# The last tile of a gate projection issued among the first score groups of a stick-breaking attention

## What is computed

```python
def _sb_layer(x, k, v, norm_g, w_in, w_out):
    q, g = split(_rms(x, norm_g) @ w_in)        # two halves of 1024 columns
    o = _stick_breaking(q, k, v)                # 16 heads of 64
    return x + (o * silu(g)) @ w_out

# stick-breaking, per block of 128 query rows, mask: kpos < qpos
z = q @ k.T * scale
log_beta, log_1mb = log_sigmoid(z), where(mask, log_sigmoid(-z), 0)
suffix = reversed_cumsum(log_1mb) - log_1mb
a = where(mask, exp(log_beta + suffix), 0)
o = a @ v
```

## Time and profile before

| | |
|---|---|
| median of 3 runs | 2435.43 us (2435.22 to 2443.52) |
| the profiled execution | 2447.21 us; span 2445.4 us, mean granted TensorE clock 0.99 |
| PE busy | 2346.2 us (96%) |
| DVE busy | 1492.6 us (61%) |
| ACT busy | 994.6 us (41%) |
| POOL busy | 209.0 us (9%) |
| DMA | 116.02 MB, mean 47 GB/s |

### The profile page before, as it was taken

How to read it: one execution, slowest core, us unless ns; L and a number is a source line. 1 busy time by engine, 2 the same in 40 slices (tenths; PEclk the granted TensorE clock), 3 DMA queues, 4 the chain that set the end, 5 groups by cost and what they waited for, 6 DMA issues and landing times.

```text
span 2445.4 us, 30312 instructions
## 1 busy us (share of the span) xinstructions
PE 2346.2 (96%) x12882; PEld 1255.3 (51%) x12882; DVE 1492.6 (61%) x1880; ACT 994.6 (41%) x1498; POOL 209.0 (9%) x258
## 2 busy tenths in 40 slices
PE   7999989999999999999999977899999999989999
PEld 5445444444444444444544455654444446777764
DVE  6898855644644455587732388865534405988951
ACT  5245344221212122433332578842323215878841
POOL 0001030000000000533301101022000000000000
PEclk9999999999999999999999999999999999999999
DMA  4010000201110101003111000021131200010021
GB/s 183 35 70 35 1 35 35 103 35 69 41 63 35 69 35 69 32 6 138 35 69 35 34 2 1 1 104 35 69 138 35 70 1 1 1 36 1 1 87 52
DMA packets 50343, 116.02 MB, mean 47 GB/s; under 512 B 2402, under 2 KB 7835, under 8 KB 49824
## 3 DMA queue, kind: packets, MB, share of 16 engines
q1 hardware_dynamic: 48472, 105.40, 12.1%
q10 hardware_dynamic: 1736, 8.68, 0.9%
HBM read 101.49 MB, written 12.58 MB: 47 GB/s over the span
## 4 chain that ended last, share of the span: by engine, by line
PE 79%; DVE 12%; ACT 7%; issue 1%; DMA 1%; POOL 0%; SPq 0%; DVEq 0%; ACTq 0%
PE PS L72 76%; PE PS L75 4%; ACT RG L81 3%; DVE RG L107 2%; DVE R L93 2%; DVE mx L110 2%; DVE R L101 2%; ACT OV L84 2%; DVE RG L101 1%; DVE RG L93 1%; DMA RG<-in_a_w_in 1%; ACT R L81 1%; DVE scl L110 1%; DVE oss L110 1%; ACT mx L81 0%
## 5 line engine op out<-in xcount | busy, mean ns | idle before, releaser
L72 PE MATMUL PS<-R,RG 128*128 128x512 f16 (+1 forms) x5472 | 1164.7, 374 | 7.5 <-DVE R L93 3.4
L72 PEld LDWEIGHTS PS<-R,RG 128*128 128x128 f16 (+1 forms) x5472 | 542.6, 103 | 625.3 <-issue 10.2
L72 PE MATMUL PS<-RG,R 128*128 128x512 f16 x2880 | 632.6, 380 | 3.6 <-DVE R L101 3.1
L72 PEld LDWEIGHTS PS<-RG,R 128*128 128x128 f16 x2880 | 281.9, 98 | 335.4 <-issue 5.2
L81 ACT ACTIVATE R<-PS,scl 128x512 f32<-128x512 f32 (+1 forms) x192 | 126.7, 686 | 700.4 <-PE PS L72 630.9
L101 DVE SCALAR_TENSOR_TENSOR R<-PS,scl,R 128x512 f32<-128x512 f32 (+1 forms) x208 | 148.6, 745 | 147.2 <-PE PS L72 122.6
L107 DVE TENSOR_TENSOR_SCAN RG<-RG 128x127 f32<-128x127 f32 (+7 forms) x128 | 168.4, 1342 | 92.1 <-ACT RG L81 91.9
L101 DVE SCALAR_TENSOR_TENSOR RG<-RG,scl 128x4096 f16<-128x4096 f32 (+2 forms) x52 | 190.6, 3664 | 54.4 <-ACT RG L81 54.4
L72 PE MATMUL PS<-R,OV 128*128 128x64 f32 (+2 forms) x1456 | 198.8, 279 | 7.2 <-DVE R L93 4.8
L81 ACT ACTIVATE RG<-RG,scl 128x4096 f16<-128x4096 f32 (+2 forms) x52 | 158.6, 3050 | 89.1 <-DVE scl L113 89.1
L110 DVE TENSOR_REDUCE scl<-RG 128x1 f32<-128x4096 f32 (+2 forms) x39 | 155.0, 3975 | 64.4 <-DMA RG<-in_a_w_in 25.3
(11 more groups left out here) (128 smaller groups left out, 1554.4 us busy)
## 6 DMA issues: line engine op xcount, KB each, us to landing
RG<-in_w_ff SPq DMA_DIRECT2D x16, 2048.0 KB, 8.2
RG<-in_a_w_in SPq DMA_DIRECT2D x8, 2048.0 KB, 8.6
xspill<-R ACTq DMA_DIRECT2D x2, 4096.0 KB, 15.6
RG<-in_w_kv SPq DMA_DIRECT2D x4, 2048.0 KB, 8.0
RG<-in_b_w_in SPq DMA_DIRECT2D x4, 2048.0 KB, 8.0
RG<-in_w_in SPq DMA_DIRECT2D x3, 2048.0 KB, 7.9
R<-in_x SPq DMA_DIRECT2D x8, 512.0 KB, 8.0
RG<-in_w_out SPq DMA_DIRECT2D x2, 2048.0 KB, 7.8
```

The costliest lines, as they stand in the source:

```text
L72: return self.engine.matmul(*a, **k) if self.engine else Nothing()
```

## The change

The seven first gate tiles stay where they are; the seventh is pinned to banks 6 and 7. The eighth tile's halves are issued in banks 6 and 7 behind the scores of groups 1 and 2, so that the order on PE is scores 0, scores 1, `("g2", 7, 0)`, scores 2, `("g2", 7, 1)`, scores 3, and then transposes of group 0. As the weights of tile 38 are still read while groups 0 and 1 are at work, their 1 - beta goes to `EB[2]` and `EB[3]` (`kept(u)`), and ACT waits for joins 0 and 1 before it writes the beta of groups 2 and 3 there.

On ACT the eighth tile's two Silu stand behind the beta of group 2, the first copy, `turned(0, 0)`, right behind them, then 1 - beta of group 3, copy (0, 1), beta of group 3, copies (1, 0), (1, 1) and (2, 0). On DVE the gating of group 0 stands behind the join of group 3 rather than ahead of its scans. The loops are the same from group 4 on.

```diff
-            for t in range(NT):
+            for t in range(NT - 1):
                 for c in range(2):
-                    product_n(38 + c, t, ("g2", t, c))
+                    product_n(38 + c, t, ("g2", t, c), bank=6 + c if t == NT - 2 else None)
...
             scores([0])
-            for u in range(N + 2):
-                if u + 1 < N:
+            scores([1])
+            product_n(38, NT - 1, ("g2", NT - 1, 0), bank=6)
+            scores([2])
+            product_n(39, NT - 1, ("g2", NT - 1, 1), bank=7)
+            for u in range(1, N + 2):
+                if u == 1:
+                    scores([3])
+                elif 2 < u < N - 1:
                     if sb_groups[u + 1][0] < 4:
                         scores([u + 1])
                     elif u % 2:
```

```diff
+        def kept(u):
+            return EB[2 + u] if u < 2 else EC[u % 3]
...
+            for u in range(N + 3):
+                if u != 3:
+                    gated(u - 3)
...
-                        back = EC[u % 3][:, w * x + 1:w * x + w][:, ::-1]
+                        back = kept(u)[:, w * x + 1:w * x + w][:, ::-1]
...
                     e.tensor_tensor(eb, eb, ec, ALU.mult).then_inc(*sig("joined_b").up(u))
+                if u == 3:
+                    gated(0)
```

```diff
-                turned(u - 2, 1)
+                if u == 3:
+                    turned(0, 1)
+                if u > 3:
+                    turned(u - 2, 1)
                 if u < N:
+                    if u in (2, 3):
+                        e.wait_ge(*sig("joined_b").at(u - 2))
...
-                turned(u - 1, 0)
+                if u == 2:
+                    gate_silu(NT - 1)
+                    turned(0, 0)
+                if u == 3:
+                    turned(1, 0)
+                    turned(1, 1)
+                if u > 2:
+                    turned(u - 1, 0)
```

More of the change, by code:

```diff
@@ L1822, in vector, with gated @@
             N = len(sb_groups)
-            for u in range(N + 3):
-                if u >= 3:
-                    i, hs = sb_groups[u - 3]
+            def gated(u):
+                if u >= 0:
+                    i, hs = sb_groups[u]
                     if hs[-1] % 8 == 7:
@@ L1843, in vector @@
                     w = width(i)
-                    eb, ec = by_head(EB[u % 4], u)[:, :, 0:w - 1], by_head(EC[u % 3], u)[:, :, 1:w]
+                    eb, ec = by_head(EB[u % 4], u)[:, :, 0:w - 1], by_head(kept(u), u)[:, :, 1:w]
                     e.wait_ge(*sig("beta").at(u))
@@ L2378, in scalar, with gate_silu @@
             e.dma_start(OV[:, 2048:2176], A["c_ms"]).then_inc(*sig("mask_in").up(by=16))
-            for t in range(NT):
+            def gate_silu(t):
                 for c in range(2):
@@ L2385, in scalar @@
                         *banks.empty([key], sig("bank_act"), *key))
+            for t in range(NT - 1):
+                gate_silu(t)
             def gate_high(i):
@@ L2420, in scalar @@
                         e.wait_ge(*sig("joined_b").at(u - 3))
-                    e.activation(by_head(EC[u % 3], u), sb_scores(u), ACT.Sigmoid, scale=nsc[:, g:g + 1]).then_inc(
+                    e.activation(by_head(kept(u), u), sb_scores(u), ACT.Sigmoid, scale=nsc[:, g:g + 1]).then_inc(
                         *sig("one_minus").up(u))
-                turned(u - 2, 1)
+                if u == 3:
+                    turned(0, 1)
+                if u > 3:
+                    turned(u - 2, 1)
                 if u < N:
+                    if u in (2, 3):
+                        e.wait_ge(*sig("joined_b").at(u - 2))
                     if u >= 4:
```

## The result

The changed kernel is slower: 2451.18 us, median of 20 runs (2440.76 to 2458.66), against 2441.76 us for the kernel before over 20 runs (2435.22 to 2449.37). The ratio is 1.0035, with a 95% interval of 1.0024 to 1.0046. The forecast was 2435.2 us in a range of 2429.5 to 2442. Part of the miss is the base: the 3 runs shown of the kernel before had a median of 2435.4, its 20 runs one of 2441.8. The change itself costs 9.4 us between the medians, where -0.2 was forecast. The size of 9.4 is a loose one: the 20 runs of the changed kernel lie in two bands, nine from 2440.8 to 2445.3 and eleven from 2450.7 to 2458.7, and the median is the low end of the upper band. The means differ by 8.4 us.

What follows compares the result with a forecast made beforehand. PE was taken as the bound, 79% of the span, with idle and slow-clock time behind the gates. A shift of -3.3 + 0.43 L, L = 7.3, gave -0.2 us: 2435.4 - 0.2 = 2435.2 us, range 2429.5 to 2442.

Steps and rivals of the forecast that it cites:

- The stall at 2013: PE at gate tile seven waits for bank 6, held until the sixth tile's second Silu: 1.4 us of new idle.
- the gap at the knot: PE stands 2.2 us ahead of transposes (1, 0), behind ACT's table load, 1 - beta of group 3 and copy (0, 1).
- The law for the shift: Up to the second gating, shift is -3.3 + 0.43 L us, L being time at 1.2 GHz; kept to the stage's end.
- The term L: Time at 1.2 GHz behind the knot after the change: 7.3 us, from 2046.9 to 2054.2, giving a shift of -0.2 us.
- The base: The shift, worked out on a profiled execution of 2447.21 us, was carried unchanged to the median of 2435.4 us.
- the forecast case: The clock falls again behind the knot: L of 5 to 10.2 us, time 2434.3 to 2436.5 us; chance 0.55.
- The third: Rival: the 1.4 us stall at bank 6 brings its own clock fall; with L = 10.2, +2.7, 2438.1 us; chance 0.12.
- The clock holds: Rival: behind the knot the clock holds or falls for one short time; 2432.1 to 2433.5 us; chance 0.2.
- Later falls come out otherwise: Rival: slow windows at 2130, 2180 and 2230 cost 5.8 us, may vanish or double; 2429.4 to 2441 us; chance 0.1.
- A switch holds ACT for longer than its row: Rival: a table load on ACT holding it twice its 1.28 us would make the time 2436.5 us; chance 0.03.
- The moved gating: On DVE, group 0's gating behind group 3's join finds its products done at about 2049 to 2051; cost none.
- The far end: Behind the attention, gated block 0's first transposes start 0.9 us later for bank 7; cost 0 to 0.1, taken as 0.

Runs made afterwards that it cites:

- e3: The changed kernel with ten idle matmuls of 512 columns in PE's gap of 2.33 us ahead of transposes (1, 0); 2441.42 us, ratio 0.9998.
- e12: The kernel before, not edited, run again for a second trace; its profiled execution took 2438.2 us.
- e13: The kernel before, not edited, run again for a third trace; its profiled execution took 2439.8 us.
- e1: The changed kernel with the two banks of the seventh gate tile exchanged, so that PE has no stall at bank 6; 2455.21 us, ratio 1.0050.
- e5: The changed kernel with ten idle matmuls in the gap ahead of transposes (1, 0) and seven in each of four later gaps; 2441.37 us, ratio 0.9999.
- e7: The changed kernel with Sigmoid for Silu in the last gate tile, so without the two added table loads (last 128 rows not the reference's); 2443.81 us, ratio 1.0011.
- e8: The changed kernel with copies (0, 1), (1, 0), (1, 1) ahead of the second table load and group 0's gating again ahead of group 3's scans; 2440.84 us, ratio 1.0002.
- e2: The changed kernel with copies (0, 1), (1, 0) and (1, 1) on ACT ahead of the second table load and group 3's Sigmoids; 2448.49 us, ratio 1.0031.
- e6: The kernel before with eight idle matmuls in the gap ahead of transposes (0, 0) and seven in each of four later gaps; 2438.65 us, ratio 0.9993.
- e4: The kernel before with eight idle matmuls in its gap of 1.90 us ahead of transposes (0, 0); 2444.94 us, ratio 1.0011.
- e11: The changed kernel, not edited, run again for a second trace; its profiled execution took 2453.2 us.
- e15: The changed kernel, not edited, run again for a fourth trace; its profiled execution took 2455.3 us.
- e10: e8 with the seventh gate tile's banks exchanged as in e1, and seven idle matmuls in each of four later gaps; 2438.09 us, ratio 0.9982.

## Why the prediction was wrong

**The order of the work: right.** The stall at 2013 was forecast at 1.4 and is 1.36; the wait ahead of scores 0 went; scores and products stand where they were put; the gap at the knot was forecast at 2.2 and is 2.33; transposes (1, 0) are 0.25 us later than before, forecast 0.35; the first table load hides, the second does not. Only the small wait of 0.15 to 0.55 us ahead of transposes (1, 1) did not come.

**The law for the shift: right for the changed order, and its start right by luck.** At L = 0 a shift of -3.3 us against the profiled kernel before was forecast; e3 has 108.8 - 112.4 = -3.6. But two errors cancel in it. The forecast took 3.8 us for what the slow stretch costs the kernel before (8.8 us at 0.43), and some 0.5 us for what the new order costs at full clock. The traces have 112.4 - 109.5 = 2.9 us for the first and a gain of 0.7 for the second. (The terms given for the way to the second gating also add up to 7.4 us with the wait of 0.5, not 7.1; e3, which has no such wait, takes 6.9.) In the order before, the 10.3 us at 1.2 GHz so cost 0.28 us each, and the 3.4 us of e12 cost nothing, for its way is that of e13. The price of 0.43 us for each us at 1.2 GHz holds for the changed order over the whole range: (117.7 - 108.8) / 20.5 = 0.43, (114.9 - 108.8) / 13.7 = 0.45, and for e1, with 1.36 us less of stall, (120.7 - 107.5) / 30.7 = 0.43.

**The term L: wrong, and it is the step that failed.** "I take a fall ... and the return at the time it comes today, 2054.2: L = 7.3". Forecast were 7.3 us, measured 20.5. The start came 1.0 us after the one taken, at 2046.0 us on PE against 2046.9 - 1.9 = 2045.0 forecast. The return came at 2066.4, where 2052.3 was forecast. I took the end of the stretch from one trace of another order of work, in which it turned out to be the longest of three (10.3, 3.4, 0), and bounded it by that: "L of 5 to 10.2". With 20.5 the law gives -3.3 + 8.8 = +5.5 us, and against a usual run of the kernel before, way 109.5, the changed kernel's 117.7 is +8.2. The medians differ by 9.4; that the two numbers are near each other proves little, as the falls behind the way and the two bands stand in the medians too.

**The base.** Of the 16.0 us between 2435.2 and 2451.2, 6.3 are the base: two of the three runs shown were among the lowest of the 20. The same choice of one sample stands behind "today": the profiled execution had a fall that two more traces have hardly or not at all. A shift worked out against 112.4 was carried over to a median of runs whose way is likelier 109.5. Against 109.5 the same law has no gain left to give but 0.7 us at full clock, and the forecast case would have been +2.7 us (112.4 - 0.2 - 109.5): slower, the other sign.

**The rivals.** The third, a fall longer than the forecast one, had the right side and 0.12. But its place was the stall at bank 6, and e1 shows that to be wrong. "The clock holds" had 0.2 for the likeness with the first attention, whose gap of 1.71 us left the clock alone. That did not carry over: here 1.90 us was followed by a fall in two of three traces, 2.33 in all four. Nor was the likeness safe by itself: behind the same gap of 1.71 us in the first attention, the transposes take 0.79 to 1.01 us instead of 0.63 in four of all 17 traces (e5, e7, e8, e12). "Later falls come out otherwise" was right as a mechanism: 0 to 27.3 us at 2130 in kernels that do the same work there. "A switch holds ACT for longer than its row" did not show: the switch on the path cost 1.4 us (e7).

**The moved gating.** "Costs no one anything" was right. No run shows that it brings anything either: e8 has it back in its old place with a way of 109.1 us against 108.8 in e3, but differs in its copies too. It is a risk (e2, 4.90 us).

**The far end: right.** The transposes of block 0 wait 0.78 us for bank 7, and the output product starts no later for it. PE at the end of the attention, which answers the earlier trace rows:

```profile
2345.64 1.97 PE L75 MATMUL PS<-ident,R 128*128 128x128 f32 x16 [0.78 <-DVE R L93]
2349.01 5.35 PE L72 MATMUL PS<-RG,R 128*128 128x512 f16 x24 [1.41 <-DVE R L101]
```

Not foreseen was that this splits the gap of 2.23 us in two. The 24 matmuls behind it take 5.35 us, not 7.04. That is not shown to come of the split: with the gap whole they take 7.04 us in two traces (the kernel before and e6) and 5.35 in three (e4, e12 and e13), and with it split 5.35 in all twelve. The row of e12:

```profile
2336.52 5.35 PE L72 MATMUL PS<-RG,R 128*128 128x512 f16 x24 [2.23 <-DVE R L101]
```

**Still open** is why the slow stretch ends when it does. In both orders PE runs the same transposes, products and scores behind transposes (1, 0), nearly without a wait; counted from the start of those transposes, the fall begins 3.3 us later in the changed order (1.9 us behind it, against 1.4 ahead of it) and ends 13.5 us later (22.3 against 8.8). That the changed order has the longer stretch is seen in four traces against three without overlap (e11 to e15); what in it decides is not.

## What to carry to other kernels

In a place like this knot (short transposes and products behind the gap; whether it is their lightness that matters was not tested), cost a gap not by its idle time but by the slow stretch that may follow: here 0 to 30 us long, at 0.43 us for each us at 1.2 GHz in the changed order and 0 to 0.28 in the order before. Break a gap of 2 us in two by the order of the copies, or fill it; and before a shift is worked out against one trace, ask whether its slow stretches are those of the median run.

Read the clock column beside the busy share: a PE at 10.00 of 10 us can be at half speed.

## What the runs showed that was not expected

- PE stayed at 1.2 GHz for 20.5 us (changed) and 30.7 us (e1) while it was busy without a wait. The Trainium skill, "TensorE: Matmul & The Clock Gate", section "What's actually happening", has the idle state throttled and activity release it; here two windows with 10.00 of 10 us busy stayed at 0.50 (e1).
- A denser lead-in gave a longer slow stretch, not a shorter one: e1, without the stall of 1.36 us, 30.7 us (one trace) against 13.7 to 20.5 (four).
- Where the longest gap at the knot was 0.68 to 1.16 us, no fall followed in any of eight traces (e3 to e10); at 1.90 us one followed in two of three, at 2.33 us in all five, and at 4.90 us in the one (e2).
- The runs of the kernel before follow their mean granted clock. Of 88 timed beside the experiments, those at 0.994 or more took 2435 to 2441 us, and those at 0.990 or less 2444 to 2450.
